# Another order of panel work, stores and angle tables in the first layer of a two-block model

## The reference

```python
def even_layer(hn, rel_bias, w_in, w_out, ...):
    q, k, v, gate_a, u, gate_b = split_cols(hn @ w_in, EVEN_SPLITS)
    q, k = rms_norm(q by heads of 64), rms_norm(k by heads of 64)
    att = swa_sink_attention(q, k, v, sinks, rel_bias) * silu(gate_a)   # window of 128
    ssm = s5_mixer(u, log_dt, a, b, c, d_skip, glu) * silu(gate_b)
    return concatenate([att, ssm]) @ w_out

def s5_mixer(...):      # 32 groups of 16 channels, 64 complex states each
    ab = exp(a * dt)                           # magnitude and angle
    bu = einsum(u, bb)
    x_t = ab * x_(t-1) + bu_t                  # over the 1024 tokens
    y = Re(einsum(x, c)) + d_skip * u
    y = gelu(y);  h = y @ glu_w + glu_b
    return h[..., :512] * sigmoid(h[..., 512:])
```

## Time and profile before

| | |
|---|---|
| median of 3 runs | 2120.17 us (2119.67 to 2125.78) |
| the profiled execution | 2119.67 us, span 2118.4 us |
| PE busy | 2027.6 us, 96% of the span, 9260 matmuls |
| DVE, ACT, POOL busy | 1396.0, 878.3, 644.1 us |
| granted TensorE clock, mean | 0.985 |
| PE busy from 0 to 60 us | 50.36 us |
| PE busy from 60 to 75 us | 14.71 us |
| PE busy from 75 to 97 us | 22.00 us |
| PE busy from 97 to 242 us | all 145 us (six stretches) |
| PE busy from 242 to 266 us | 23.96 us |

### The profile page before, as it was taken

The page is one execution under the profiler, slowest core; times in us unless marked ns, Lnnn a source line. Parts: engine busy times, 40 slices in busy tenths (PEclk is TensorE's granted clock), DMA queues, the critical chain, the costliest instruction groups (busy, mean ns, idle before and its releaser), DMA issues.

```text
span 2118.4 us, 24438 instructions
## 1 busy us (share of the span) xinstructions
PE 2027.6 (96%) x9260; PEld 1540.5 (73%) x9260; DVE 1396.0 (66%) x2137; ACT 878.3 (41%) x1540; POOL 644.1 (30%) x482
## 2 busy tenths in 40 slices
PE   8999988999999999899999999999999999999997
PEld 6778865887557676566678787888787767778885
DVE  7668576222346889454517699899998746784639
ACT  5333286233445763244412333444224545362331
POOL 3676500542101111354535100000003444235443
PEclk9999998999999999999999999999999999999999
DMA  6422332332400112311042311121123111555322
GB/s 257 133 58 77 114 112 72 120 137 75 134 20 31 41 60 80 99 41 41 30 160 91 117 41 50 40 70 60 60 103 121 58 63 64 200 188 219 110 80 109
DMA packets 72429, 197.91 MB, mean 93 GB/s; under 512 B 11182, under 2 KB 20559, under 8 KB 71800
## 3 DMA queue, kind: packets, MB, share of 16 engines
q1 hardware_dynamic: 72168, 196.35, 27.1%
q10 hardware_dynamic: 144, 0.00, 0.0%
HBM read 152.89 MB, written 46.71 MB: 94 GB/s over the span
## 4 chain that ended last, share of the span: by engine, by line
PE 55%; DVE 19%; ACT 5%; issue 3%; POOL 2%; DMA 2%; SPq 0%; DVEq 0%; ACTq 0%; POOLq 0%
PE psum L262 52%; DVE m L2849 6%; PE psum L265 2%; DVE m L2870 2%; POOL m L307 1%; DMA m<-in_w 1%; DVE m L317 1%; DVE m L452 1%; DVE m L527 1%; DVE m L536 1%; ACT m L297 1%; DVE m L2082 1%; PE psum L1955 1%; ACT m L1405 1%; DVE m L2259 1%
## 5 line engine op out<-in xcount | busy, mean ns | idle before, releaser
L262 PE MATMUL psum<-m,m 128*128 128x512 f32 (+8 forms) x8420 | 1923.6, 394 | 53.6 <-DVE m L2206 10.8
L262 PEld LDWEIGHTS psum<-m,m 128*128 128x128 f32 (+4 forms) x8420 | 1445.8, 187 | 505.0 <-issue 157.4
L307 POOL TENSOR_TENSOR m<-m,m 128x1024 fp32r<-128x1024 f32 (+1 forms) x124 | 313.8, 2534 | 1030.8 <-ACT m L297 1030.6
L297 ACT ACTIVATE m<-m 128x1024 fp32r<-128x1024 f32 (+2 forms) x166 | 173.5, 1049 | 358.1 <-PE psum L262 251.3
L2849 DVE SCALAR_TENSOR_TENSOR m<-m,m,m 128x1024 f32<-128x1024 f32 x240 | 310.3, 1294 | 6.3
L265 PE MATMUL psum<-m,m 128*128 128x128 f32 x784 | 112.6, 280 | 23.4 <-ACT m L1420 9.4
L265 PEld LDWEIGHTS psum<-m,m 128*128 128x128 f32 x784 | 91.5, 144 | 45.4 <-ACT m L1420 17.9
L2082 DVE TENSOR_SCALAR_CACHE_REDUCE m<-m,m 128x896 bf16<-128x896 f32 (+4 forms) x130 | 102.7, 847 | 1.0
L2206 DVE CUSTOM_DVE_ANT_0 m<-psum,m 128x128 f32<-128x128 f32 (+3 forms) x64 | 48.2, 755 | 55.5 <-POOL m L2407 21.8
L2407 POOL TENSOR_TENSOR m<-m,m 128x384 f32<-128x384 f32 (+5 forms) x48 | 72.2, 1523 | 11.7 <-DVE m L2206 11.7
L2312 ACT ACTIVATE m<-m,m 128x1024 bf16<-128x1024 f32 (+1 forms) x62 | 64.1, 1037 | 23.6 <-DVE m L2109 23.6
(11 more groups left out here) (305 smaller groups left out, 1641.6 us busy)
## 6 DMA issues: line engine op xcount, KB each, us to landing
m<-in_w SPq DMA_DIRECT2D x164, 512.0 KB, 3.5
scr_hscr<-m SPq DMA_DIRECT2D x4, 2048.0 KB, 6.6
m<-scr_hscr SPq DMA_DIRECT2D x4, 2048.0 KB, 10.9
scr_turned<-scr_strip SPq DMA_DIRECT2D x8, 575.5 KB, 12.1
m<-in_x SPq DMA_DIRECT2D x4, 1024.0 KB, 8.1
scr_gscr<-m SPq DMA_DIRECT2D x16, 256.0 KB, 4.1
m<-in_x SPq DMA_DIRECT2D x2, 2048.0 KB, 8.0
m<-scr_turned SPq DMA_DIRECT2D x8, 512.0 KB, 3.6
```

Of the source, the lines that this page charges most:

```text
L262: return self.nc.tensor.matmul(out, lhsT, rhs, start=start, stop=stop, skip_group_check=True)
L297: k.nc.scalar.activation(k.hi[SLOT[i]][:, 0:kk * n], k.raw[i % 2][:, 0:kk * n], ACT.Copy).then_inc(*k.up("w_hi", i))
L307: k.nc.gpsimd.tensor_tensor(lo, raw, hi.bitcast(F32), ALU.subtract).then_inc(*k.up("w_lo", i))
```

## The change

No instruction is added or removed. What moves:

1. **SP.** The four stores of u alternate with panels 6 to 9. Before, the order was panel 6, two stores, panel 7, two stores, the loads of u, the strips, panels 8 and 9.
2. **ACT.** The copy of the row scale for the second half stands ahead of panel 5, not behind it.
3. **POOL.** The low parts of panels 5, 6 and 7 stand in a row ahead of `narrow(0)`. Before, 6 stood behind `narrow(0)` and 7 behind `powers(0)`.
4. **DVE.** The angle steps of groups 2 to 7 move from part 2 of the group before to part 0 of their own group, behind `outputs(n-1)`. Their scratch is `E.M1`, no longer `E.Y`, and they wait for PE's outputs of the group before.

```diff
@@ vector_even
-        if n > 1:
-            dve.wait_ge(*at("y_out", n - 2))
+            dve.wait_ge(*at("s5_Y_ps", n - 1))
         V.tensor_tensor(E.TS, bc(E.TH8[:, gs], 2, 128), bc(E.KS, 1, 4), ALU.mult).then_inc(*k.one("s5_turn"))
-        angle_in_turn(k, "s5_turn", E.TS, E.Y if n > 1 else E.M1, ("s5_turned", n))
+        angle_in_turn(k, "s5_turn", E.TS, E.M1, ("s5_turned", n))
...
         if part == 0 and n:
             outputs(n - 1)
-        if part == 0 and n < 2:
+        if part == 0 and n < 8:
             tables(n)
         if part == 1:
             states(n)
-        if part == 2 and 0 < n < 7:
-            tables(n + 1)
@@ scalar_even
     act_panel(k, 4)
-    act_panel(k, 5)
     root(1)
-    act_panel(k, 6)
-    act_panel(k, 7)
+    for m in range(1, 4):
+        act_panel(k, 4 + m)
@@ pool_even
-    pool_panel(k, 5)
+    for m in range(1, 4):
+        pool_panel(k, 4 + m)
...
     narrow(0)
-    pool_panel(k, 6)
...
             powers(n)
-            if s == 0:
-                pool_panel(k, 7)
@@ sync_even
-    sp_panel(k, 6)
-    store_u(0)
-    store_u(1)
-    sp_panel(k, 7)
-    store_u(2)
-    store_u(3)
+    for m in range(4):
         sp.wait_ge(*at("u", m, 1))
         S.dma_start(d["uscr"][128 * m:128 * m + 128], E.ut[m]).then_inc(...)
+        sp_panel(k, 6 + m)
...
     S.dma_start(E.rawb, ...).then_inc(*up("band_raw", by=16))
-    sp_panel(k, 8)
-    sp_panel(k, 9)
```

More of the change, by code:

```diff
@@ L1573, in pool_even @@
     narrow(0)
-    pool_panel(k, 6)
     for s, (kind, m, half) in enumerate(E.slots):
-        n, part = ssm_turn(s)
         if kind in ("q", "kk", "v") and half:
@@ L1580, in pool_even @@
             pool_panel(k, 14 + m)
+        n, part = ssm_turn(s)
         if part == 0 and n < 8:
             powers(n)
-            if s == 0:
-                pool_panel(k, 7)
             if n < 7:
@@ L1649, in sync_even @@
     S.dma_start(E.rbt[0:32], d["rb"]).then_inc(*up("onehots", by=16))
-    def store_u(m):
+    for m in range(4):
         sp.wait_ge(*at("u", m, 1))
         S.dma_start(d["uscr"][128 * m:128 * m + 128], E.ut[m]).then_inc(*up(f"u_out{m}", by=16, also=[("u_out", m)]))
-    sp_panel(k, 6)
-    store_u(0)
-    store_u(1)
-    sp_panel(k, 7)
-    store_u(2)
-    store_u(3)
+        sp_panel(k, 6 + m)
     def load_u(n):
```

## The result

The changed kernel takes 2138.75 us in the median of four runs (2136.71 to 2140.62), against 2119.92 for the kernel before. Over all runs of the two the ratio is 1.0074, with an interval of 1.0061 to 1.0087. That is 15.7 us of 2120 (12.9 to 18.4). The forecast was 7.8 us and its range ended at 15: the direction was right, the size off by a factor of two.

What follows compares the result with a forecast made beforehand. PE, busy in 96% of the span, was taken as the bound, so new waits are paid in full. Opening 4.8 plus slots 3.0 made 7.8 us on 2120.0, forecast 2127.8, range 2123.5 to 2135.

Steps and rivals of the forecast that it cites:

- opening, to group 1: PE waits for narrow(0), then at the states for ACT's copies behind the later strip store: 4.8 us together.
- group 5 (slot 16): Behind slot 16 PE waits for the norms' bank until DVE's first product on V ends: 1.5 us.
- group 6 (slot 19): Behind slot 19 the same wait of PE for the norms' bank, held by DVE's first product on V: 1.5 us.
- a rival of 10%: The opening's upper end, under which a loss of clock was mentioned without a number; 2131.2 us, chance 10%.
- the first wait: In the opening, PE waits for narrow(0)'s weights behind POOL's low parts of panels 6 and 7: 3.4 us.
- the second: In the opening, PE waits again at the states for ACT, held by the strip store: about 2 us more.
- The opening hidden: Panels land in 3.5 us or less, DVE's gain is whole; only the slots cost 3.0 us: 2123.0, chance 10%.
- the slots hidden: PE comes too late to see the bank waits; only the opening costs 4.8 us: 2124.8, chance 12%.
- No slower: PE takes its opening delay back at a later wait free of the chain; the whole 7.8 goes: 2120.0, chance 5%.
- The recurrence as the bound: Spread K or scan's result comes too late for PE; six groups cost about 1 us more each: 2133.8, chance 13%.
- The opening's upper end: DVE is not earlier and panels land late, so the opening costs 8.2 in place of 4.8: 2131.2, chance 10%.

Runs made afterwards that it cites:

- after_fill: The changed kernel with unread matmuls filling PE's waits, 20 ahead of group 0's transposes, 12 and 4 behind slots 16 and 19: 1.0044 against the kernel before.
- after_gate_first: The changed kernel with SP's gate stores ahead of the spread of K in the same slot: 1.0059 against the kernel before, 12.5 us.
- groups_2347: The kernel before with only the angle steps of groups 2, 3, 4 and 7 moved to part 0 of their own group: 0.9999, -0.2 us.
- act_only: The kernel before with only ACT's part, the row scale ahead of panel 5: 0.9997, -0.6 us.
- opening_only: The changed kernel with DVE's angle steps put back to part 2 of the group before: 1.0025 against the kernel before, 5.3 us.
- slots_only: The kernel before with only DVE's part, angle steps of groups 2 to 7 in part 0 of their own group: 1.0039, 8.3 us.

## Why the prediction was wrong

Against the sum, in the traces' us (the order is read from `after_fill`, where the clock is out of it):

| term | predicted | order alone | the changed kernel |
|---|---|---|---|
| opening, to group 1 | 4.8 | 5.7 | 7.5 |
| group 5 (slot 16) | 1.5 | 3.3 | 6.5 |
| group 6 (slot 19) | 1.5 | 1.2 | 2.9 |
| to the attention | 7.8 | 10.2 | 16.8 |

- **The step that failed: the sum had no term for the clock.** The prediction read "a loss of clock would come on top of this", named it inside a rival of 10%, and gave it no number. Each wait was priced at its own length. The runs showed 6.4 us of 15.7 (6.6 of 16.8) behind the waits, three quarters or more of what was missing. Rows for a price were in the trace of before, outside of the stretch that was summed: the wait of 9.66 us at 886 with 0.54 behind it, and nearer in size a wait of 2.26 us, behind which the clock is at 0.50 from 315 to 320 and 16 matmuls take 3.98 us, where they take 2.15 at 301.62:

```profile
315.30 1.97 PE L265 MATMUL psum<-m,m 128*128 128x128 f32 x8 [2.26 <-DVE m L1150]
317.19 3.98 PE L262 MATMUL psum<-m,m 128*64 128x256 f32 x16
```

  The page's clock in forty slices is no help: the line is the same before and after, and losses of 3 us do not show in it.
- **The opening, mis-sized by 0.9.** With the clock kept (`after_fill`) every link was as drawn: DVE 2.4 us earlier, the first store at 57.20, panel 9 in front of the loads of u, the strips at 75.85 (74.8 forecast), PE at the states at 80.67 (80.0 forecast). The landing of panel 7, 7.8 us for an assumed 4.5, made the first wait 5.3 us for 3.4 and took the second down to 1.15 for 2. The range of 3.5 to 5.4 was too narrow for a load issued behind two stores and another load.
- **Group 5, mis-sized by 1.8.** Group 1's rows were a fair template for the angle steps, but group 1 has no gate. In group 5 DVE first stood in a gate's product, for a store behind the late spreads on SP. The prediction counted the late spreads only for PE's use of them, and not for what else stands behind them in SP's queue. `after_gate_first` shows 1.5 us of it. Group 6 came out at 1.1 to 1.2 for 1.5.
- **What held.** The place of each wait (the second of the opening only with the clock kept); no wait in groups 2, 3, 4 and 7 (`groups_2347`, 0.9999); nothing for ACT's part (`act_only`, 0.9997); PE never waits for spread K or the scan's result, so the recurrence does not become the bound; nothing clear of the noise was given back later (16.8 us at the attention in the trace, 15.7 in the whole runs). The Trainium skill (SBUF — State Buffer, Who interferes with whom) is borne out at L1018: the same product took 0.68 us at 48.69, with POOL idle, for 2.88 beside it.
- **The rivals.** The opening hidden (2123.0) and the slots hidden (2124.8) each fall to the run of the half that they call hidden: `opening_only` costs 5.3 us (2.8 to 7.8), `slots_only` 8.3 (5.3 to 11.2). No slower falls likewise. The recurrence as the bound (2133.8) is nearest to the measured time, but by its number only: PE waits for no spread and no scan, and four of its six groups cost nothing. The opening's upper end (2131.2) had the late panel right and DVE wrong.

**Open.** What decides the level behind a given wait is not settled, nor why it fell at 64 us in six executions without a wait. Neither is the loss past 283 us in the profiled execution (8.4 us, and the 11 us between the fastest and the slowest run): no experiment took that part of the program.

## What to carry to other kernels

On a kernel where the matrix engine never rests, a new wait costs its length and then a second amount for the clock behind it, which here was anything from nothing to 3.2 us for waits of 1.1 to 5.3 us, each read from single traces. Put both ends into the sum, and look in the trace of before for any wait with the granted clock behind it, in whatever stage, as a price. Where a wait can't go, a few matmuls that nobody reads may buy back the second amount. When a step is moved, walk down the queues of all that it issues, and price what stands behind it there, stores of a few tenths of a us too.

## What the runs showed that was not expected

- **One wait, several prices.** The same piece of 80 matmuls behind slot 16 or 19 took 16.2, 17.8 or 19.4 us. Behind a wait of 1.14 us it took 16.19 in `slots_only` and 17.79 to 17.84 in three other kernels, behind 1.68 us 16.21 or 19.40, behind 3.2 us 17.79 or 19.41. The wait's length alone does not tell which. The Trainium skill (TensorE: Matmul & The Clock Gate, Part 1, What's actually happening) says that the number of slow matmuls at a kernel's start differs between runs of one kernel; these rows show a like spread in the middle of one, though between kernels and in one trace of each. The piece at 62.8 us (5.7 or 7.3 us) shows it with no wait at all: up to there `groups_2347` is the kernel before.
- **A slow clock can hide a wait.** Behind the wait of 5.3 us PE came to the states so late that the next wait, 1.15 us at full clock, was gone. From the wait's end to 80 us the clock was low for 5.9 us; half of it is 3.0, and 1.8 reached the time.
- **A load among stores.** Panels landed in 3.5 us in the median, and in 5.4 and 7.8 us between the stores of u.
